# Filter sums on TensorE, a new order of the opening loads, delta gates in the low-rank products, one set of decay sums

## The chip, the cores and the metric

The kernel runs on one core of one Trainium2 chip. The metric is the device time of one execution in microseconds; less is better. TensorE (PE) multiplies, VectorE (DVE) and ScalarE (ACT) work on elements, GpSimd (POOL) here issues DMAs, and SyncE (SP) issues most of the weight loads.

## The reference, cut to what matters

256 tokens of width 1024 go through two blocks of two layers each. All is float32.

```python
def hybrid_layer(x, mem_n, ...):            # first block, layers 0 and 1
    h = rmsnorm(x, norm_mix)
    (a_x, a_b, a_c, d_q, d_k, d_v, i_q, i_k, i_w, ...) = split_cols(h @ w_in)
    y_a = a_b * causal_conv3(a_c * a_x, conv_w)
...
def ab_prepare(t, w_in, ...):               # second block, layer 0, on latent and context tokens
    gq, gk, gv, gz, ga, gb, lq, lk, lv, lg, llr = jnp.split(t @ w_in, AB_SPLITS, axis=-1)
    gate = jnp.einsum('bldr,drk->bldk', heads(llr, 2, GLA_GATE_RANK), gla_gate_w) + gla_gate_b
    gdn_g = -jnp.exp(a_log) * jax.nn.softplus(heads(ga, 2, GDN_HEADS) + dt_bias)
    gdn_beta = jax.nn.sigmoid(heads(gb, 2, GDN_HEADS))
...
def run_gdn(q, k, v, g, beta, s0, emit):    # chunks of 64 tokens
    gc = jnp.cumsum(g, axis=-1)
...
def hyena_filters(l, w1, b1, ..., filt_out):# second block, layer 1
    hdn = jnp.sin(fr * (z @ w1 + b1)); hdn = jnp.sin(fr * (hdn @ w2 + b2)); hdn = jnp.sin(fr * (hdn @ w3 + b3))
    h = (hdn @ filt_out).reshape(l, 2, HY_ORDER, D_MODEL)      # forward and backward filter
    return h * window
def long_conv(z, h_fwd, h_bwd, skip):       # two-sided, h_bwd[0] is not used
```

With a spectrum that uses the symmetry, the long convolution needs the sum and the difference of the forward and the backward filter, with row 0 of the backward one taken as zero.

## The kernel before, in words

One program per engine is written out by hand; each waits on semaphores that name what it needs (`reached("...")`), and each mark names what is done. The sources of TensorE, ScalarE and VectorE for the first block start at lines 318, 935 and 1263, for the second block at 1954, 2433 and 2702; `whole_program` (line 3232) holds SP's and POOL's lists and the short prologue of ScalarE.

Weights come in panels: `panel_plan` and `second_panels` give their order, and a ring of six slots of 1 MB holds them. A panel waits until the panels that had its slots are used. A panel of 512 columns (2 MB) takes two slots, the first three being a_x0, small0 and a_c0. Where a product is split into high and low parts, ScalarE copies the high part of a quarter panel (`prepared`) and VectorE subtracts to the low part (`lows`). `Banks.take` hands out four PSUM banks in turn; a new user waits until the old result is read.

Opening. SP issues the two tiles of x, the whole constant table (identity, masks, ones, inverse frequencies: 1.28 MB), half of the small parameter rows, positions, mem, and then the panels in their order (lines 3326 to 3345). ScalarE issues the other half of the parameter rows before it does anything else (3416). TensorE first turns the four stacks of parameter rows into columns (583), VectorE copies them (1403), and only then does the norm of x begin: sum of squares on ScalarE (950), root on VectorE (1302 to 1312), scaling (1318), transposes (556), gain (1348). Then come a_x, small (two results) and a_c. Behind the first products VectorE makes the sine table's arguments (`constants_of_dve`) and the norm of mem.

Second block, layer 0. After lv TensorE makes the low-rank rows llr of both token sets (48 rows of output) and then, with tokens as rows, the 16 columns of the delta gates (gab), for each token tile and each of eight k. lq, the gates, lk, gk and so on follow. `decays_summed(s)` multiplies gab with triangular and block matrices of ones, for each token set and tile; VectorE copies (`decays_copied`), ScalarE takes the exponential.

Second block, layer 1. Three filter layers (`filter_pe`, `filter_act`, `filter_dve`) run inside the FFN steps 4, 6 and 8 of layer 0. `filters(n)` (2334) is called after hy0 and again after hy5: for both column halves and both token tiles it makes the forward and the backward filter, with 64 rows in. `filtered(n)` (3084) on VectorE multiplies each with the window into a temporary, adds and subtracts them to hs and hd, zeroes the backward row 0 and adds the skip row. `filter_spectrum(n)` needs both; with n = 1 the spectra Z of the tokens are made between `filters` and `filter_spectrum`. POOL loads what the filters need once the attention residual of layer 0 is done (3380 to 3400) and then the modulation weights (3360).

## Time and profile before

| what | value |
| --- | --- |
| median of 3 runs | 2268.71 us (2268.51 to 2268.97) |
| profiled execution, device time | 2271.08 us |
| profiled execution, span | 2269.3 us, mean granted clock 0.975 |
| TensorE busy | 2175.8 us, 96% of the span |
| VectorE busy | 1432.4 us, 63% |
| ScalarE busy | 809.5 us, 36% |
| chain that ended last | PE 84%, DVE 10%, ACT 2%, DMA 2%, issue 1% |

A row of busy times gives the stretch and its length, then the busy us and the number of instructions of PE, PEld, DVE, ACT and POOL, the granted clock, the DMA share and GB/s.
### The profile page before, as it was taken

How to read it: one execution, taken by the hardware profiler on the slowest of the kernel's cores; microseconds unless marked ns; L12 is line 12 of the kernel's file. 1: busy time of each engine (PE TensorE's matmuls, PEld its weight loads, DVE VectorE, ACT ScalarE, POOL GpSimd, SP SyncE). 2: the span in 40 equal slices, each digit the busy share in tenths (PEclk: the TensorE clock that was granted, in tenths of full speed). 3: DMA queues.
4: the chain of work that ended last, by engine and by line, in shares of the span. 5: the costliest groups of instructions: out<-in, count | busy, mean ns of one | idle time of the engine just before them, and what ended most of it. 6: DMA issues, size and time to landing. Idle time of an engine off the chain costs nothing.

```text
span 2269.3 us, 36109 instructions
## 1 busy us (share of the span) xinstructions
PE 2175.8 (96%) x15182; PEld 1866.2 (82%) x15182; DVE 1432.4 (63%) x2369; ACT 809.5 (36%) x1026; POOL 57.4 (3%) x79
## 2 busy tenths in 40 slices
PE   6999999999999999999999998989999989999997
PEld 5997899799999878979997887886699967557996
DVE  4791677599568537758975385665477662645454
ACT  3453642334336446204442353220444312104342
POOL 0000000000000000000100000000100000000000
PEclk9999999999999989999999998998999999999999
DMA  6433347776464333777972212010686433204562
GB/s 211 178 132 129 111 166 251 235 247 215 134 193 162 130 112 112 254 266 246 300 250 84 94 56 75 2 39 1 197 278 223 149 121 111 74 10 154 181 186 74
DMA packets 207766, 348.59 MB, mean 154 GB/s; under 512 B 20642, under 2 KB 111561, under 8 KB 207220
## 3 DMA queue, kind: packets, MB, share of 16 engines
q1 hardware_dynamic: 192704, 290.89, 38.3%
q0 software_dynamic: 14624, 55.31, 7.1%
q8 instruction: 120, 1.97, 0.3%
q14 instruction: 42, 0.34, 0.1%
q10 hardware_dynamic: 276, 0.08, 0.0%
HBM read 345.21 MB, written 1.05 MB: 153 GB/s over the span
## 4 chain that ended last, share of the span: by engine, by line
PE 84%; DVE 10%; ACT 2%; DMA 2%; issue 1%; SPq 0%; POOL 0%; DVEq 0%; ACTq 0%
PE psum L447 35%; PE psum L841 29%; PE psum L484 16%; DVE G L1348 2%; DMA ring<-in_w_in_dram 1%; PE psum L819 1%; PE psum L542 1%; DVE wide_room L1348 1%; PE psum L556 1%; DMA x1tok<-in_mod_w_dram 1%; DVE x L1348 1%; DVE ring_low L1348 0%; ACT A L944 0%; DVE A L1728 0%; DVE A L1348 0%
## 5 line engine op out<-in xcount | busy, mean ns | idle before, releaser
L1218 DVE TENSOR_TENSOR ring_low<-ring,high_weights 128x2048 fp32r<-128x2048 f32 x124 | 284.3, 2292 | 132.7 <-ACT high_weights L1211 129.9
L841 PE MATMUL psum<-high_rows,high_weights 128*128 128x256 f32 x1280 | 361.6, 283 | 0.7 <-ACT xn L1239 0.7
L841 PE MATMUL psum<-high_rows,ring_low 128*128 128x256 f32 x1280 | 360.9, 282 | 0.0
L484 PE MATMUL psum<-mix_rows_high,ring_low 128*128 128x256 f32 x960 | 270.9, 282 | 0.0
L447 PE MATMUL psum<-hT,ring 128*128 128x128 f32 (+1 forms) x1552 | 255.8, 327 | 10.0 <-DVE x L1348 3.4
L447 PEld LDWEIGHTS psum<-hT,ring 128*128 128x128 f32 x1552 | 230.8, 196 | 33.6 <-issue 6.5
L841 PEld LDWEIGHTS psum<-high_rows,high_weights 128*128 128x128 f32 x1280 | 240.9, 188 | 3.5 <-issue 2.2
L841 PEld LDWEIGHTS psum<-high_rows,ring_low 128*128 128x128 f32 x1280 | 243.3, 190 | 0.0
L1211 ACT ACTIVATE high_weights<-ring 128x2048 fp32r<-128x2048 f32 x124 | 237.9, 1919 | 8.3 <-DMA ring<-in_ffn_w_dram 2.9
L484 PEld LDWEIGHTS psum<-mix_rows_high,ring_low 128*128 128x128 f32 x960 | 183.0, 191 | 0.0
L841 PE MATMUL psum<-x2T_low,high_weights 128*128 128x256 f32 x640 | 180.1, 281 | 0.0
L841 PE MATMUL psum<-yT_low,high_weights 128*128 128x256 f32 x640 | 179.8, 281 | 0.0
L1728 DVE SCALAR_TENSOR_TENSOR A<-A,silu_c 128x256 f32<-128x256 f32 x336 | 163.0, 485 | 12.0
L484 PE MATMUL psum<-mix_rows_high,work_high 128*128 128x256 f32 x560 | 160.4, 286 | 0.0
L484 PE MATMUL psum<-xn_low,work_high 128*128 128x256 f32 x560 | 156.9, 280 | 0.0
L841 PE MATMUL psum<-high_weights,high_act 128*128 128x512 f32 x352 | 140.9, 400 | 1.8 <-DVE ring_low L1218 1.4
L841 PE MATMUL psum<-ring_low,high_act 128*128 128x512 f32 x352 | 138.3, 393 | 0.0
L841 PE MATMUL psum<-high_weights,xn_low 128*128 128x512 f32 x352 | 137.5, 391 | 0.0
L841 PEld LDWEIGHTS psum<-x2T_low,high_weights 128*128 128x128 f32 x640 | 121.4, 190 | 0.5
L841 PEld LDWEIGHTS psum<-yT_low,high_weights 128*128 128x128 f32 x640 | 120.4, 188 | 0.7
L447 PE MATMUL psum<-ring,hT 128*128 128x512 f32 (+2 forms) x320 | 120.9, 529 | 0.0
L484 PE MATMUL psum<-mix_rows_high,mix_high 128*128 128x256 f32 x400 | 116.7, 292 | 3.4 <-DVE ring_low L1348 3.4
(443 smaller groups left out, 3776.2 us busy)
## 6 DMA issues: line engine op xcount, KB each, us to landing
ring<-in_w_in_dram SPq DMA_DIRECT2D x36, 2048.0 KB, 7.8
ring<-in_ffn_w_dram SPq DMA_DIRECT2D x66, 1024.0 KB, 5.4
ring<-in_ffn_w_up_dram SPq DMA_DIRECT2D x44, 1024.0 KB, 6.2
A<-in_mod_w_dram POOLq DMA_DIRECT2D x40, 1024.0 KB, 8.0
ring<-in_ffn_w_down_dram SPq DMA_DIRECT2D x22, 1024.0 KB, 4.9
ring<-in_w_lift_dram SPq DMA_DIRECT2D x16, 1024.0 KB, 9.2
ring<-in_ab_w_in_dram SPq DMA_DIRECT2D x7, 2048.0 KB, 8.2
ring<-in_hy_w_in_dram SPq DMA_DIRECT2D x6, 2048.0 KB, 8.1
```

Of the source, the lines that this page charges most:

```text
L447: return pe.eng.matmul(out, lhsT, rhs, start=(k == 0), stop=(k == n - 1))
L484: ins = pe.eng.matmul(out, lhs[a], rhs[b], start=first and n == 0, stop=last and n == 2)
L542: ins = pe.eng.transpose(b[:, i * P:(i + 1) * P], src(i), ident[:, :])
L556: ins = pe.eng.transpose(b[:, i * P:(i + 1) * P], rows[:, t, k * P:(k + 1) * P], ident[:, :])
L819: ins = pe.eng.matmul(b[:, 2 * c + which:2 * c + which + 1], mod_acc(i)[:, which, c * P:(c + 1) * P], consts["ones"][:, 0:1], start=True, ...
L841: ins = pe.eng.matmul(out, lhs[a], rhs[b], start=first and n == 0, stop=last and n == 2)
L1211: a.eng.activation(high, whole, ACT.Copy).then_inc(*a.mark(f"w_hi/{l}.{i}"))
L1218: v.eng.tensor_tensor(low, whole, high.bitcast(F32), ALU.subtract).then_inc(*v.mark(f"w_lo/{l}.{i}"))
L1348: e.tensor_tensor(dst, a, b, op).then_inc(*v.mark(label, also))
L1728: v.eng.scalar_tensor_tensor(acc, w[:, k, :], s, acc, ALU.mult, ALU.add).then_inc(*v.mark(f"mod_acc/{i}" if done else None))
```

## The change

- Filters: the third filter layer is made twice, in rows 0 to 63 and 64 to 127, the backward copy's first column is zeroed, and a second version has the lower half negated. Forward and backward filter weights lie above each other, so that one matmul with 128 rows in gives the sum and another the difference. VectorE multiplies each with the window, and adds the skip row. POOL issues three more small DMAs for the second copy.
- Opening: SP loads x tile 0, the gains of the mix norms, the identity, x tile 1, panel a_x0, half of the parameter rows, panel small0, the inverse frequencies, positions, panel a_c0, mem, the rest of the table and the other panels. ScalarE issues its half after the squares of x. TensorE turns the gains alone first, and all stacks after a_x. The constants move ahead of a_c's parts, and the norm of mem behind them.
- Delta gates: their 16 weight columns join the low-rank panel, so that the product has 80 rows of output; after lq a product with a 16 by 16 identity brings them to token rows.
- Decay sums: five matmuls for both token sets and tiles, and one set of copies and one exponential.

```diff
@@ -575,13 +575,10 @@
-        pe.wait_ge(*reached("params/all"))
-        pe.wait_ge(*reached("params_b/all"))
-        for i, n in enumerate(top["stack_rows"]):
-            label = f"stackT_ready/{i}"
-            b = take(label)
-            ins = pe.eng.transpose(b[:, 0:n], top["stacks"][0:n, i, :], ident[0:n, 0:n])
-            ins.then_inc(*pe.mark(label))
+        pe.wait_ge(*reached("gains/all"))
+        b = take("stackT_ready/gains")
+        ins = pe.eng.transpose(b[:, 0:16], top["stacks"][0:16, 0, :], ident[0:16, 0:16])
+        ins.then_inc(*pe.mark("stackT_ready/gains"))
...
@@ -604,6 +601,13 @@
+            if l == 0:
+                pe.wait_ge(*reached("params/all"))
+                pe.wait_ge(*reached("params_b/all"))
+                b = take("stackT_ready/all")
+                for i, n in enumerate(top["stack_rows"]):
+                    ins = pe.eng.transpose(b[:, i * P:i * P + n], top["stacks"][0:n, i, :], ident[0:n, 0:n])
+                ins.then_inc(*pe.mark("stackT_ready/all"))
...
@@ -629,6 +633,8 @@
+            if l == 0:
+                pe.wait_ge(*reached("table/rest"))
...
@@ -1028,14 +1034,13 @@
             if l == 0:
-                for t in range(MT):
-                    a.wait_ge(*reached(f"xn/mix0.{t}"))
-                    squared("mem", t, mem_in, "mem_in/0")
+                top["act_loads"]()
...
-            prepared(l, None, 0)
+            if l:
+                prepared(l, None, 0)
...
@@ -1043,6 +1048,9 @@
                      [f"read a_x_ready/{l}.{u}"])
             if l == 0:
                 constants_of_act()
+                prepared(l, None, 0)
+                for t in range(MT):
+                    squared("mem", t, mem_in, "mem_in/0")
             b = take(f"small_ready/{l}.0")
...
@@ -1422,24 +1424,33 @@
+                else:
+                    v.wait_ge(*reached(f"x_in_{t}/0"))
...
-                if t == 0 and l:
-                    norm_out(f"mix{l}", 0, PA[:, 8 * l:8 * l + 8])
-            for t in range(MT):
-                if t or not l:
-                    norm_out(f"mix{l}", t, PA[:, 8 * l:8 * l + 8])
+                if (l, t) == (0, 0):
+                    label = "stackT_ready/gains"
+                    e.tensor_copy(PA[:, 0:16], take(label)[:, 0:16]).then_inc(*v.mark("columns/gains", ["read " + label]))
+                    v.wait_ge(*v.own())
+                norm_out(f"mix{l}", t, PA[:, 8 * l:8 * l + 8])
...
+            if l == 0:
+                b = take("stackT_ready/all")
+                for i, n in enumerate(top["stack_rows"]):
+                    lo = 0 if i else 16
+                    e.tensor_copy(top["columns"][i][:, lo:n], b[:, i * P + lo:i * P + n]).then_inc(
+                        *v.mark(f"columns/{i}", ["read stackT_ready/all"] if i == 3 else []))
+                    v.wait_ge(*v.own())
+            if l == 0:
+                constants_of_dve()
...
-                constants_of_dve()
-                for t in range(MT):
-                    norm_rows("mem", t, mem_in)
-
+                v.wait_ge(*reached("table/rest"))
+                norm_rows("mem", 0, mem_in)
...
@@ -1451,6 +1462,8 @@
+                if l == 0 and u == 1:
+                    norm_rows("mem", 1, mem_in)
...
@@ -1927,26 +1945,36 @@
+        if i == 2:
+            v.eng.memset(hdn[FR:, 2, 0:1], 0.0).then_inc(*v.mark())
+            v.wait_ge(*v.own())
+            for rows, sign in ((slice(0, FR), 1.0), (slice(FR, P), -1.0)):
+                v.eng.tensor_scalar(hdn[rows, 3, :], hdn[rows, 2, :], sign, None, ALU.mult).then_inc(
+                    *v.mark("hdn_pairs/0" if sign < 0 else None))
+                v.wait_ge(*v.own())
...
@@ -2077,17 +2105,17 @@
-        def decays_summed(s):
-
-            pe.wait_ge(*reached(f"g/{s}"))
-            b = take(f"dec_ready/{s}")
-            for t in range(MT):
-                for d in range(2):
-                    mm(b[:, 32 * t + 4 * d:32 * t + 4 * d + 4], consts["tri"][:, d, :], gab[:, s, t, 4 * d:4 * d + 4])
-                mm(b[:, 32 * t + 8:32 * t + 16], consts["chunk_ones"], gab[:, s, t, 0:8])
-                for c in range(2):
-                    ins = mm(b[:, 32 * t + 16 + 8 * c:32 * t + 24 + 8 * c], consts["chunk_sel"][:, c, :], gab[:, s, t, 0:8])
-            ins.then_inc(*pe.mark(f"dec_ready/{s}"))
+        def decays_summed():
+
+            for s in SL:
+                pe.wait_ge(*reached(f"g/{s}"))
+            b = take("dec_ready/all")[:, 0:128].rearrange("p (s t c) -> p s t c", s=2, t=2)
+            for d in range(2):
+                mm(b[:, :, :, 4 * d:4 * d + 4], consts["tri"][:, d, :], gab[:, :, 0:2, 4 * d:4 * d + 4])
+            mm(b[:, :, :, 8:16], consts["chunk_ones"], gab[:, :, 0:2, 0:8])
+            for c in range(2):
+                ins = mm(b[:, :, :, 16 + 8 * c:24 + 8 * c], consts["chunk_sel"][:, c, :], gab[:, :, 0:2, 0:8])
+            ins.then_inc(*pe.mark("dec_ready/all"))
...
@@ -2114,16 +2142,16 @@
-                ins = mm(b[0:48, 0:SEQ], w[:, k, 16:64], src[s][:, k, :], k, KD)
-            ins.then_inc(*pe.mark(f"llr_ready/{s}"))
-        for s in SL:
-            b = take(f"gab_ready/{s}")
-            for t in range(MT):
-                for k in range(KD):
-                    ins = mm(b[:, t * 16:t * 16 + 16], src[s][:, k, t * P:(t + 1) * P], w[:, k, 0:16], k, KD)
-            ins.then_inc(*pe.mark(f"gab_ready/{s}", [used] if s else []))
+                ins = mm(b[0:80, 0:SEQ], w[:, k, 0:80], src[s][:, k, :], k, KD)
+            ins.then_inc(*pe.mark(f"llr_ready/{s}", [used] if s else []))
         w, used = panel("lqk")
         transposed("lq", w, [], 1, 2, 0)
+        for s in SL:
+            pe.wait_ge(*reached(f"llrT/{s}"))
+            b = take(f"gab_ready/{s}")
+            for t in range(MT):
+                ins = mm(b[:, t * 16:t * 16 + 16], narrow[64:80, s, t * P:(t + 1) * P], ident[64:80, 64:80])
...
@@ -2337,13 +2364,13 @@
-                    pe.wait_ge(*reached("hdn/2"))
+                    pe.wait_ge(*reached("hdn_pairs/0"))
...
-                        ins = mm(b, hdn[:, 2, t * P:(t + 1) * P], filt[:, (2 * n + half) % 2, s * HALF:(s + 1) * HALF])
+                        ins = mm(b, hdn[:, 2 + s, t * P:(t + 1) * P], filt[:, half, :])
...
@@ -2556,7 +2583,7 @@
-            copy(llrT[:, s, :], take(f"llr_ready/{s}")[0:48, 0:SEQ], f"llrT/{s}", [f"read llr_ready/{s}"])
+            copy(narrow[:, s, :], take(f"llr_ready/{s}")[0:80, 0:SEQ], f"llrT/{s}", [f"read llr_ready/{s}"])
...
@@ -2588,9 +2615,8 @@
-        for s in SL:
-            a.wait_ge(*reached(f"dec/{s}"))
-            copy(decx[:, s, :, :], decx[:, s, :, :], f"decx/{s}", func=ACT.Exp)
+        a.wait_ge(*reached("dec/all"))
+        copy(decx[:, :, :, :], decx[:, :, :, :], "decx/all", func=ACT.Exp)
...
@@ -2811,14 +2837,14 @@
+        def decays_copied():
+
+            label = "dec_ready/all"
+            e.tensor_copy(dec[:, :, :, :], take(label)[:, 0:128].rearrange("p (s t c) -> p s t c", s=2, t=2)).then_inc(*v.mark(None, ["read " + label]))
...
-            e.tensor_copy(decx[:, s, :, :], dec[:, s, :, :]).then_inc(*v.mark())
+            e.tensor_copy(decx[:, :, :, :], dec[:, :, :, :]).then_inc(*v.mark())
             v.wait_ge(*v.own())
-            tt(decx[:, s, :, 8:16], dec[:, s, :, 8:16], dec[:, s, :, 0:8], ALU.subtract, f"dec/{s}")
+            tt(decx[:, :, :, 8:16], dec[:, :, :, 8:16], dec[:, :, :, 0:8], ALU.subtract, "dec/all")
...
@@ -3089,16 +3114,11 @@
-                    tt(tmp2[:, 0, :], take(l0), window[:, t, cc], ALU.mult, None, ["read " + l0])
-                    tt(tmp2[:, 1, :], take(l1), window[:, t, cc], ALU.mult, None, ["read " + l1])
-                    if t == 0:
-                        e.memset(tmp2[0:1, 1, :], 0.0).then_inc(*v.mark())
-                        v.wait_ge(*v.own())
-                    tt(hs[:, t, cc], tmp2[:, 0, :], tmp2[:, 1, :], ALU.add)
+                    tt(hs[:, t, cc], take(l0), window[:, t, cc], ALU.mult, None, ["read " + l0])
                     if t == 0:
                         tt(hs[0:1, 0, cc], hs[0:1, 0, cc], skip[0:1, n, cc], ALU.add)
-                    tt(hd[:, t, cc], tmp2[:, 0, :], tmp2[:, 1, :], ALU.subtract, f"filtered/{n}.{half}.{t}",
-                       [f"h_sums/{n}"] if half and t else [])
+                    tt(hd[:, t, cc], take(l1), window[:, t, cc], ALU.mult, f"filtered/{n}.{half}.{t}",
+                       ["read " + l1] + ([f"h_sums/{n}"] if half and t else []))
...
@@ -3322,18 +3342,8 @@
-            for t in range(MT):
-                sp.eng.dma_start(x[:, t, :], io["x"][0][t * P:(t + 1) * P, :]).then_inc(*sp.loads(f"x_in_{t}/0"))
-            sp.eng.dma_start(const_sb[:, :], io["shape_table"]).then_inc(*sp.loads("const/ident"))
-            for dst, src in loads_of_params[0::2]:
-                sp.eng.dma_start(dst, src).then_inc(*sp.loads(f"params/{len(marks.at)}"))
-            sp.eng.dma_start(top["pos"][:, :], io["positions"][0].partition_broadcast(P)).then_inc(*sp.loads("pos/0"))
-            for l in range(DEPTH):
-                sp.eng.dma_start(top["gb_out"][:, l, :], io["hgrn_out_norm"][l].partition_broadcast(P)).then_inc(*sp.loads(f"pos/gb{l}"))
-            marks.at["params/all"] = ("params", marks.count["params"])
-            marks.at["pos/all"] = ("pos", marks.count["pos"])
-            sp.eng.dma_start(first["mem_in"], io["mem"][0].rearrange("(t p) d -> p t d", p=P)).then_inc(*sp.loads("mem_in/0"))
...
@@ -3341,6 +3351,28 @@
+            sp.eng.dma_start(x[:, 0, :], io["x"][0][0:P, :]).then_inc(*sp.loads("x_in_0/0"))
+            for dst, src in gains_of_mix:
+                sp.eng.dma_start(dst, src).then_inc(*sp.loads(f"gains/{len(marks.at)}"))
+            marks.at["gains/all"] = ("gains", marks.count["gains"])
+            sp.eng.dma_start(const_sb[:, 0:P], io["shape_table"][:, 0:P]).then_inc(*sp.loads("const/ident"))
+            sp.eng.dma_start(x[:, 1, :], io["x"][0][P:2 * P, :]).then_inc(*sp.loads("x_in_1/0"))
+            panel_asked(plan[0])
+            for dst, src in loads_of_params[0::2]:
+                sp.eng.dma_start(dst, src).then_inc(*sp.loads(f"params/{len(marks.at)}"))
+            panel_asked(plan[1])
+            sp.eng.dma_start(const_sb[:, -2:], io["shape_table"][:, -2:]).then_inc(*sp.loads("pos/inv_freq"))
+            sp.eng.dma_start(top["pos"][:, :], io["positions"][0].partition_broadcast(P)).then_inc(*sp.loads("pos/0"))
+            for l in range(DEPTH):
+                sp.eng.dma_start(top["gb_out"][:, l, :], io["hgrn_out_norm"][l].partition_broadcast(P)).then_inc(*sp.loads(f"pos/gb{l}"))
+            marks.at["params/all"] = ("params", marks.count["params"])
+            marks.at["pos/all"] = ("pos", marks.count["pos"])
+            panel_asked(plan[2])
+            sp.eng.dma_start(first["mem_in"], io["mem"][0].rearrange("(t p) d -> p t d", p=P)).then_inc(*sp.loads("mem_in/0"))
+            sp.eng.dma_start(const_sb[:, P:-2], io["shape_table"][:, P:-2]).then_inc(*sp.loads("table/rest"))
+            for name in plan[3:]:
+                panel_asked(name)
...
@@ -3384,8 +3416,11 @@
+            pool.eng.dma_start(second["hyw"][:, 3, :], io["hy_pos_w3_2"][0]).then_inc(*pool.loads("params3/w2_again"))
+            pool.eng.dma_start(second["hyb"][FR:, 2:3], io["hy_pos_b3_2"][0].rearrange("(p a) -> p a", a=1)).then_inc(*pool.loads("params3/b2_again"))
+            for s in range(2):
+                pool.eng.dma_start(second["hyb"][s * FR:(s + 1) * FR, 3:4], io["hy_freq_2"][0].rearrange("(p a) -> p a", a=1)).then_inc(*pool.loads(f"params3/freq{s}"))
...
@@ -3412,9 +3447,13 @@
-            for dst, src in loads_of_params[1::2]:
-                act.eng.dma_start(dst, src).then_inc(*act.loads(f"params_b/{len(marks.at)}"))
-            marks.at["params_b/all"] = ("params_b", marks.count["params_b"])
+            def act_loads():
+
+                for dst, src in loads_of_params[1::2]:
+                    act.eng.dma_start(dst, src).then_inc(*act.loads(f"params_b/{len(marks.at)}"))
+                marks.at["params_b/all"] = ("params_b", marks.count["params_b"])
+
+            top["act_loads"] = act_loads
...
```

## Rows read from the trace of the kernel before

**Rows 1.** Chain of waits in order of time: start us, us, what.
```profile
11.32 13.74 DMA ring<-in_w_in_dram
```

**Rows 2.** Busy time in two stretches of the opening.
```profile
25.11:53.77 28.66, 28.66 (x201) 27.83 (x202) 16.19 (x37) 13.30 (x20) 0.00 (x0) 1.00 0.59 179
15.00:20.00 5.00, 1.17 (x4) 0.65 (x4) 3.50 (x15) 0.00 (x0) 0.00 (x0) 1.00 0.99 387
```

**Rows 3.** Timeline, opening: start us, us, engine line op, [idle before <-releaser].
```profile
8.18 1.28 ACT L950 ACT_TABLE_LOAD   x1 [8.18 <-issue]
...
9.48 1.06 ACT L950 ACTIVATE yT<-x 128x1024 f32<-128x1024 f32 x1
...
15.41 1.17 PE L583 MATMUL psum<-const_sb,ytok 104*128 104x104 f32 x4 [15.41 <-DMA ytok<-in_hy_conv_w_dram]
...
17.13 0.15 DVE L1302 TENSOR_SCALAR st<-st 128x1 f32<-128x1 f32 x1
...
20.02 1.97 PE L556 MATMUL psum<-const_sb,xn 128*128 128x128 f32 x8 [3.43 <-DVE xn L1318]
...
22.86 1.42 DVE L1348 TENSOR_TENSOR hT<-psum,columns 128x512 f32<-128x512 f32 x2
...
43.47 0.29 DVE L1409 CAST A<-pos 128x256 f32<-128x256 int32 x1
...
49.89 0.17 DVE L1352 TENSOR_SCALAR lbc<-lbc 128x8 f32<-128x8 f32 x1 [2.26 <-ACT lbc L1001]
```

**Rows 4.** Timeline, TensorE, projections of the second block.
```profile
1259.28 3.75 PE L447 MATMUL psum<-ring,cT 128*128 128x16 f32 x32
1262.87 6.68 PE L447 MATMUL psum<-ring,hT 128*128 128x16 f32 x32
1269.39 9.16 PE L447 MATMUL psum<-hT,ring 128*128 128x256 f32 x32
1278.48 1.14 PE L447 MATMUL psum<-row,gla_w 16*128 16x256 f32 x8
1279.55 7.17 PE L447 MATMUL psum<-cT,ring 128*128 128x256 f32 x32
```

**Rows 5.** Busy time and granted clock (PEclk) in three stretches, columns as in rows 2.
```profile
1263.00:1273.00 10.00, 10.00 (x42) 9.28 (x42) 1.05 (x6) 0.00 (x0) 0.00 (x0) 0.51 0.01 2
...
1848.00:1851.00 3.00, 2.13 (x5) 0.78 (x4) 2.70 (x6) 0.00 (x0) 1.07 (x2) 0.89 1.05 406
...
1953.00:1963.00 10.00, 8.75 (x10) 3.35 (x11) 9.40 (x15) 0.00 (x0) 0.00 (x0) 0.50 0.02 5
```

**Rows 6.** Timeline, TensorE, decay sums and gq.
```profile
1374.84 7.80 PE L447 MATMUL psum<-gab,const_sb 128*128 128x4 f32 x40 [1.48 <-DVE G L1348]
1382.48 15.84 PE L447 MATMUL psum<-hT,ring 128*128 128x256 f32 x64
```

**Rows 7.** Timeline, first filter pass.
```profile
1848.78 1.42 DVE L1348 TENSOR_TENSOR tmp<-psum,window 128x512 f32<-128x512 f32 x2
...
1853.04 1.42 DVE L1348 TENSOR_TENSOR tmp<-psum,window 128x512 f32<-128x512 f32 x2
1853.78 3.78 PE L447 MATMUL psum<-filt,hdn 64*128 64x512 f32 x4 [1.11 <-DVE tmp L1348]
...
1857.49 4.78 PE L447 MATMUL psum<-hT,ring 128*128 128x256 f32 x14
```

**Rows 8.** Timeline, second filter pass.
```profile
1957.96 16.46 PE L447 MATMUL psum<-ztok,dft 128*128 128x512 f32 x32
...
1964.26 1.42 DVE L1348 TENSOR_TENSOR wide_room<-psum,wide_room 128x512 f32<-128x512 f32 x2 [0.72 <-PE psum L447]
```

**Rows 9.** Chain of waits, FFN of the second block's first layer.
```profile
1632.13 12.80 DMA x1tok<-in_mod_w_dram
```

**Rows 10.** Instructions on the tile x before 12 us: issue to landing.
```profile
DMA to landing us min/median/max: 3.8/4.2/4.6
```

**Rows 11.** Timeline, VectorE, decay gates of the second block.
```profile
1287.89 2.04 DVE L1353 TENSOR_SCALAR G<-psum,columns 128x256 f32<-128x256 f32 x4 [4.87 <-PE psum L447]
```

61 lines of the change are left out of this document (29 added, 32 removed).

## The prediction, made before the changed kernel was run

> **What bounds the kernel now.** I read the chain of waits first, then the timelines of the stretches that the diff touches, then the granted clock in them. The chain lies on TensorE nearly throughout, so an edit pays in two cases only: where it takes instructions off TensorE while TensorE is what the chain follows, or where it shortens a stretch in which TensorE stands. In order of time the change touches five places.
>
> The opening. The chain begins with a weight load: the panel a_x0 is issued at 11.32 and lands 13.74 us later [rows 1], and from 25.11 TensorE is busy without a gap until a_c at 53.77 [rows 2]. SP has issued x, the table and half of the small parameter rows before it. The first normed tile is there earlier, when TensorE's transposes start at 20.02 [rows 3].
>
> The gates of the second block. TensorE spends 3.75 + 6.68 us on matmuls of 16 columns, and the lq product behind them takes 9.16 us where the equal lk product takes 7.17 [rows 4]. The granted clock is 0.51, the lower level of 1.2 GHz, from 1263 to 1273, and TensorE has been busy all the time before it fell, with these narrow matmuls [rows 4, 5].
>
> The decay sums. Forty records of 4 to 8 columns take 7.80 us, and gq's 64 records behind them 15.84 us [rows 6]; twice the 7.17 of lk [rows 4] would be 14.3.
>
> The filters, twice. TensorE gets four results out, has to wait for a bank, and VectorE reads a bank only every other pair of its own instructions [rows 7, 8]. Here too the clock goes to 0.50 [rows 5].
>
> The modulation load behind POOL's row of small DMAs, 12.80 us in the chain [rows 9].
>
> **The change part by part.**
>
> Opening. TensorE's first product needs the first half of hT for tile 0 and the panel a_x0. After the change the path to hT is: x tile 0 lands 3.8 us after its issue at 0.74, at 4.5 [rows 10]. ScalarE no longer issues 19 DMAs first; it loads its table (1.28) and squares (1.06, and about 0.1 for reading the sum) [rows 3]: 7.0. The root and the scaled copy on VectorE are the stretch from 17.13 to the transposes at 20.02, 2.9 us [rows 3]: 9.9. Four transposes are half of 1.97, and one of the two gain multiplies half of 1.42 [rows 3]; with three hand-overs of some 0.07: 11.8. VectorE copies the gains while TensorE transposes. ScalarE issues its 19 DMAs after its second square and is done near 15; only its high copies of hT queue behind them, which nobody needs before a_c. The panel has 0.5 + 0.06 + 0.5 + 2 MB of x, identity and itself to pass. The queue moved 387 GB/s when it was full [rows 2]; 3.1 MB are 8.0 us from about 2.5, so it lands near 10.6 to 11.5, just ahead of hT. I take 11.9 for the start against 25.11: 13.2 us less.
>
> The four transposes of the parameter stacks, which lay in idle time, now stand between a_x and small. They took 1.17 us at the low clock [rows 3], 0.6 at the full one, and behind them TensorE waits, by my estimate, 0.15 for ScalarE to read a_x's second bank. That is 0.75 back: the opening gives 12.4.
>
> What could eat it is the work that the new order puts behind TensorE's start: the sine table, the parameter columns and the mem norm. Between start and a_c TensorE has 28.66 us of work of its own, VectorE 16.2 and ScalarE 13.3 in the same time [rows 2], so both have room. But the order in it changes: ScalarE makes the high parts of a_c only behind its constants, which need the four columns. The stacks are turned some 19 us after the start (a_x is about two thirds of the 28.66, then the 0.75); the copies took about 1.1; from the cast at 43.47 to the answer to the sigmoid are 6.4 us [rows 3]; the first part then needs a copy and a subtraction, some 2.3. That makes 28.8 us after the start, and TensorE asks at 29.4. It is close, so I keep 1 us of stall for the range. VectorE's wait for the rest of the table holds mem's norm and, behind it, the copy of dvw and the products of a_c; the table is the seventh large thing on SP's queue, 0.5 + 0.5 + 2 + 1.3 + 2 + 1 + 1.2 MB, some 28 us by the rate of [rows 2] with allowance for the narrow rows of small, and VectorE asks at about 44. Bounds for the opening: 9 (start at 14.3, 1 us of stall) to 14.
>
> Delta gates. Removed: 3.75 + 6.68 us, less overlap 1259.28 to 1269.39, 10.1 us [rows 4]. The clock no longer has this reason to fall, so lq takes 7.17 and not 9.16: 2.0 more. The product that carries them now has 80 output rows instead of 48 and the same 256 columns; a product with 128 rows of output takes 7.17/32 = 0.22 us a record, so the wider one costs nothing [rows 4]. Added: four matmuls, 8 records, with 16 rows in; the nearest row is the 8 records 16*128 of 256 columns, 1.14 us [rows 4], which bounds it above; I take 0.8. Where the path goes: VectorE waits for TensorE at 1287.89, by 4.87 us [rows 11], and then works on until TensorE waits for it, so it must start earlier too. VectorE's six operations on the gates of 16 columns now fall right before the first of these, beside the gate matmuls that it needs anyway. 12.1 - 0.8 = 11.3. Bounds 9 and 12.1. The panel small2 has one DMA more, which lands under lv's matmuls. The low-rank copy on ScalarE is done while lq runs, so the wait on it costs nothing; lq is the cover, and without it the copy would lie bare. Queued behind TensorE's wait are the gates of the context.
>
> The Trainium skill speaks against this part (TensorE: Matmul & The Clock Gate, section LDWEIGHTS): the time to load weights goes by their columns. By that, 32 columns more in 32 loads would cost 0.9 us if the loads were the limit. The record spacing in [rows 4] says that the moving side is.
>
> Decay sums. 40 records become 10. At the spacing of the 40, 7.80/40, they take 1.95: 5.85 less [rows 6]. TensorE is the chain here, and gq follows. VectorE and ScalarE have half the operations (some 0.6 us) and lie behind gq. Bounds: 4 (the clock recovers only as late as now, and gq pays) and 6.5. I take 5.8.
>
> Filters, VectorE. Each of the eight pairs loses an add, a subtract becomes the second multiply, and the temporary with its memset goes. The pair with t = 0 takes 4.26 us now (1848.78 to 1853.04), the one with t = 1 2.9; at 0.72 an instruction they take 2.2 and 1.45 after [rows 7]. All four: 14.3 against 7.3. **First pass.** The fifth matmul waits for the same read as now, at 1849.5. The seventh waits for the first read of t = 1, at 1853.75 now and at 1851.7 after. At the full clock, 0.86 us a matmul, the eight are out at 1853.6 instead of 1857.49: 3.9 us [rows 7]. What follows is TensorE's own. **Second pass.** VectorE itself is the chain: it ends the filters 7.0 us earlier, and the next thing it waits for are the first two spectra, out at 1964.26 now [rows 8]. By the same steps the eighth matmul ends at 1954.05. The 16 spectrum matmuls take 16.46 us, of which 5 at half clock [rows 5, 8], so 0.86 each; two spectra of two end at 1957.6: 6.6 us. Sum 10.5. If the clock falls as it does now, the last matmuls and the first spectra take twice as long, and the first pass gives 0.7 and the second 1.5. The filter sum now has 128 rows in instead of 64; the columns and so the time are the same.
>
> Filter layer and POOL. Layer 3 has a memset and two scalings more on VectorE, under 1 us inside an FFN step in which it has idle time. POOL issues three DMAs more ahead of the filters and the modulation load, about 0.52 us each. The load behind is 12.8 us long for 1 MB [rows 9] against 13.74 for 2 MB behind 1 MB of mem in the opening [rows 1]: its queue is behind, not its issue, so 1.6 us of issue are mostly hidden. I take 0.7, bounds 0 and 1.8.
>
> Sum: 12.4 + 11.3 + 5.8 + 10.5 - 0.7 = 39.3 us. The profiled span is 2269.3 and the device time of that execution 2271.08; the span after is 2230.0 and its time 2231.8. The median of the three runs is 2268.71, 2.4 below the profiled one, so 2229.4.
>
> **The rivals.**
>
> Clock: the pauses in the filters remain (0.9 and 0.5 us), and the clock falls as now. For it: it fell at 1851 after pauses no longer than these, with TensorE busy 2.13 of 3 us [rows 5]. Against: those matmuls used half of the rows. The filters then give 2.2: 31.0 in all, 2237.7. The Trainium skill (same page, A second HAM failure mode: psum-queue depth-cycling) has this as its rule: short idles between groups that cycle through the banks send the clock down again and again.
>
> Opening held by loads: a_x0 shares the engines with ScalarE's parameter rows and small's narrow ones, or the constants keep a_c waiting. With the start at 17 us it gives 7.3: 34.2 in all, 2234.5. The 13.74 of a 2 MB panel in [rows 1] is for it, the 387 GB/s of [rows 2] against it.
>
> Gates: the saving on TensorE is not followed by VectorE's chain, because something else (the gk panel, ScalarE's table loads) becomes late. At half of 11.3: 2235.
>
> Slower: the rest of the table lands late, VectorE stands at its wait, and everything it owes to a_b stops TensorE. To turn the sum it would have to land at about 58 + 39.3, near 97 us, on a queue with nothing to wait for ahead of it but issue. That gives 2273 or more from a landing at 102.
>
> Not doing what it says: should the narrow matmuls not be on the chain at all, [rows 11] would show VectorE busy at their end; it is idle.
>
> **How the numbers follow.** Forecast 0.62, clock 0.15, opening 0.12, gates 0.07, slower 0.03, no change 0.01. The lower end of the range takes the upper bounds of opening and clock phases (14 + 12 + 6.3 + 12, 2225) and 2 for clock changes elsewhere: 2223. The upper end covers the clock rival and half of another: 2241. A measurement here can tell about 0.2% from no change, 4.5 us; all but the last two cases are far beyond.
>
> **What would show it.** First matmul of a_x near 12; no gap before a_c; no 16-column stretch and clock 1.00 in lq; ten records of decay sums; VectorE 2.2 and 1.45 a pair in the filters, and the first product of Z near 6.6 us earlier in its stage; the modulation's first multiply no later against the residual before it. Wrong would be a start beyond 15, a VectorE wait on the table, or 0.50 in the filters for as long as now.

## The result

| kernel | median, us | range | ratio to before, 95% interval |
| --- | --- | --- | --- |
| before (beside it) | 2268.84 | 2268.51 to 2270.45, 4 runs | |
| changed | 2236.36 | 2232.31 to 2240.38, 4 runs | 0.985 [0.9832, 0.9867] |

The change gives 32.5 us, 1.4%. The forecast was 2229.4 with a range of 2223 to 2241: right in sign, inside the range, 7 us too low. The profiled execution is the quickest of the four: 2232.31 us, span 2230.4 (forecast 2231.8 and 2230.0), mean granted clock 0.984 against 0.975. The share of the clock that was not granted, times the span, says how much full-speed time TensorE was short of: it falls from 56.7 to 35.7 us, so up to 21 us of the 38.8 between the two traces is clock and not instructions taken away.

The page of the changed kernel, busy time of each engine and the share of the chain that ended last by engine:

```profile
PE 2147.5 (96%) x15097; PEld 1846.8 (83%) x15097; DVE 1419.7 (64%) x2350; ACT 808.7 (36%) x1025; POOL 59.1 (3%) x82
...
PE 83%; DVE 11%; ACT 3%; DMA 1%; issue 1%; POOL 0%; SPq 0%; DVEq 0%; ACTq 0%
```

TensorE lost 28 us of busy time and 11 us of standing. The rows that answer to those ahead of the prediction follow, place by place.

**Opening** (to rows 1 to 3). The chain of waits, from its start, then the timeline (start, duration, engine, line and operation, in brackets the idle time before and who ended it):

```profile
2.78 9.54 DMA ring<-in_w_in_dram
12.36 7.93 PE psum L447 x48
...
0.73 1.28 ACT L956 ACT_TABLE_LOAD   x1 [0.73 <-PEq L3487]
...
4.27 1.06 ACT L956 ACTIVATE yT<-x 128x1024 f32<-128x1024 f32 x1 [2.25 <-DMA x<-in_x_dram]
...
9.72 0.69 DVE L1356 TENSOR_TENSOR hT<-psum,columns 128x512 f32<-128x512 f32 x1 [1.07 <-PE psum L556]
...
30.94 7.14 PE L447 MATMUL psum<-hT,ring 128*128 128x256 f32 x32 [0.25 <-ACT work L950]
```

The first product starts at 12.36 instead of 25.11, and what starts it is the landing of a_x0: half of hT is there at 10.41, 1.95 us before. a_c starts at 41.61 instead of 53.77.

**Gates** (to rows 4, 11). Timeline of TensorE: the low-rank product of the context has 80 output rows; lq, the four small matmuls and the gate products follow without a narrow stretch. The last row is VectorE's.

```profile
1240.85 3.62 PE L447 MATMUL psum<-cT,ring 128*80 128x256 f32 x16
1244.31 10.52 PE L447 MATMUL psum<-hT,ring 128*80 128x256 f32 x48
1254.76 0.72 PE L447 MATMUL psum<-const_sb,row 16*128 16x16 f32 x5
...
1256.63 7.17 PE L447 MATMUL psum<-cT,ring 128*128 128x256 f32 x32
...
1264.97 2.04 DVE L1361 TENSOR_SCALAR G<-psum,columns 128x256 f32<-128x256 f32 x4 [4.90 <-PE psum L447]
```

**Decay sums** (to rows 6), timeline of TensorE. Ahead of gq there is a wait that the kernel before doesn't have:

```profile
1350.40 1.30 PE L447 MATMUL psum<-gab,const_sb 128*128 128x16 f32 x10 [1.48 <-DVE G L1356]
1352.79 16.95 PE L447 MATMUL psum<-hT,ring 128*128 128x256 f32 x64 [1.09 <-DVE G L1356]
```

**Filters** (to rows 5, 7, 8): timeline of the first pass, then busy time and granted clock (PEclk, the number before the DMA share) in both stretches:

```profile
1817.92 3.75 PE L447 MATMUL psum<-filt,hdn 128*128 128x512 f32 x8
1822.58 1.10 PE L447 MATMUL psum<-filt,hdn 128*128 128x512 f32 x2 [0.91 <-DVE wide_room L1356]
1823.93 2.84 PE L447 MATMUL psum<-filt,hdn 128*128 128x512 f32 x6 [0.25 <-DVE wide_room L1356]
1826.61 13.98 PE L447 MATMUL psum<-hT,ring 128*128 128x256 f32 x64
...
1816.00:1831.00 15.00, 13.84 (x56) 8.58 (x55) 11.55 (x21) 0.60 (x1) 2.10 (x4) 1.00 0.53 175
1912.00:1930.00 18.00, 16.66 (x41) 7.45 (x41) 13.98 (x23) 0.60 (x1) 0.00 (x0) 1.00 0.37 117
```

The clock no longer falls in either pass, and a matmul of 512 columns (two records) takes 0.9 us through both.

### The profile page after: what moved, and what is told of

The parts are those of the page before. It is cut to its first block, busy times and chain, and to the rows that moved or that the text cites. A ratio compares the mean times of both kernels' runs of the same rounds, so it can differ in the third digit from the quotient of the medians.

```text
span 2230.4 us, 35917 instructions
## 1 busy us (share of the span) xinstructions
PE 2147.5 (96%) x15097; PEld 1846.8 (83%) x15097; DVE 1419.7 (64%) x2350; ACT 808.7 (36%) x1025; POOL 59.1 (3%) x82
## 3 DMA queue, kind: packets, MB, share of 16 engines
q1 hardware_dynamic: 194056, 290.96, 38.8%
q8 instruction: 119, 1.95, 0.4%
## 4 chain that ended last, share of the span: by engine, by line
PE 83%; DVE 11%; ACT 3%; DMA 1%; issue 1%; POOL 0%; SPq 0%; DVEq 0%; ACTq 0%
PE psum L447 34%; PE psum L847 30%; PE psum L484 16%; DVE G L1356 2%; DMA ring<-in_w_in_dram 1%; PE psum L825 1%; PE psum L542 1%; DVE wide_room L1356 1%; PE psum L556 1%; DVE ring_low L1356 1%; DVE x L1356 1%; DMA x1tok<-in_mod_w_dram 0%; DVE A L1356 0%; ACT A L950 0%; DVE A L1741 0%
## 5 line engine op out<-in xcount | busy, mean ns | idle before, releaser
L447 PE MATMUL psum<-yT,ring 128*128 128x256 f32 x512 | 115.7, 379 | 0.0
```

The costliest lines, as they stand in the source:

```text
L447: return pe.eng.matmul(out, lhsT, rhs, start=(k == 0), stop=(k == n - 1))
```

## The leads, place by place

To say where time goes I set the start of the same VectorE instruction in two traces side by side and call the difference the lead. All leads here are against the second trace of the kernel before (label before_again, an execution of 2266.04 us), whose own times head the rows. "first" is the trace of the kernel before on which the prediction rests.

```
us   first opening gates decays decays filters changed whole  rows64 pauses panel_  split_ split_
           _only   _only _only  _again _only           _again               and_gq  and_gq only
100  -0.9   11.4   -0.4  -0.2    0.3    0.1    11.3   10.0   10.6   10.5   11.2    13.6   10.0
300  -4.1    7.1   -4.2  -0.3   -1.4    0.1     9.7    7.4    9.0    8.8    9.5    10.2    5.8
900  -5.4    5.9   -2.2  -0.3   -2.8    0.1     5.9    7.6    7.7    7.3    8.3     8.8    2.3
1290 -5.4    5.9    9.4  -0.3   -2.8    0.1    17.5   19.2   19.3   19.0   19.9    20.4   13.9
1352 -5.3    6.0    9.4  -0.3   -2.7    0.1    19.2   19.2   19.3   19.0   19.9    20.4   15.5
1425 -5.2    6.1    9.2   3.5    1.1    0.1    22.7   24.6   24.8   24.5   28.4    28.9   19.1
1550 -5.1    6.0    9.7   3.1    0.6    0.2    24.8   25.0   25.4   21.7   22.4    22.9   18.6
1810 -4.7    6.1   11.4   2.4   -2.2    0.3    22.3   26.3   27.1   23.2   24.0    24.7   19.8
1850 -4.8    6.1   11.4   2.1   -3.2    5.5    27.5   31.6   28.9   25.2   29.2    29.9   23.8
1935 -5.0    6.1   10.4   0.9   -4.6    5.5    27.5   31.6   28.9   25.2   29.2    29.9   23.8
1980 -5.1    6.1   11.0   1.5   -4.0   11.9    33.9   37.9   31.6   25.8   35.5    36.3   30.2
2260 -5.0    5.9   11.0   0.0   -5.7   11.9    33.9   36.3   30.1   25.6   34.0    36.3   30.2
```

A part of the change is a step between two rows: the opening is row 100, the gates lie between 900 and 1290, the decay sums between 1352 and 1425, the filters between 1810 and 1850 and between 1935 and 1980. The gates (11.6 to 11.7) and, with 128 rows and without VectorE's old work, the filters (5.2 to 5.3 and 6.3) take the same step in every trace that has the part, but for split_only's first pass (4.0, of which a low stretch ahead of the filter matmuls, 0.66 from 1800 to 1810, takes 1.2); the decay sums (3.5 to 5.6, 8.6 with gq moved) and the opening (10.0 to 13.6) don't. What the table shows outside the steps comes and goes between traces of one and the same kernel. One such piece helps the change: from 1290 to 1352 the column "changed" gains 1.7 us, where both traces of the kernel before have a short low stretch of the clock (0.89 from 1300 to 1315) and this one has none (1.00 from 1280 to 1300).

## The experiments

**1. The kernel before, again.** No edit.

> The kernel before once more, for a second trace of it. Against its first trace every difference is the spread of one and the same kernel. Theory 'clock': the leads wander by 3 to 5 us where the low stretches of the clock lie elsewhere (200 to 300 and 790 to 850 first of all), the stretches without a low clock take the same time within 0.1 us, and the falls at the narrow matmuls (1263) and in both filter passes (1850, 1953) are there again.

2266.04 us. The two traces of one kernel are 5 us apart, and the column "first" shows where: 3.2 us from 100 to 300, 1.3 from there to 900, nothing to speak of in the remaining 1360. The busy time and clock of two stretches, in the first trace and then in the second, hold both:

```profile
190.00:250.00 60.00, 54.90 (x251) 42.66 (x251) 19.00 (x26) 23.42 (x38) 0.00 (x0) 0.86 0.30 107
780.00:850.00 70.00, 63.92 (x306) 50.88 (x306) 21.98 (x34) 27.10 (x43) 0.00 (x0) 0.88 0.34 120
...
190.00:250.00 60.00, 55.77 (x275) 43.57 (x276) 21.64 (x37) 25.30 (x40) 0.00 (x0) 0.92 0.30 105
780.00:850.00 70.00, 63.93 (x330) 51.57 (x329) 27.24 (x43) 27.55 (x43) 0.00 (x0) 0.90 0.31 112
```

Same work, less clock. The fall at the narrow matmuls (9.39 us for lq in this trace) and those in the filter passes are there in both. The executions of the kernel before that ran beside the experiments lie between 2265.94 and 2274.76 us, their medians between 2269.03 and 2271.77. So the prediction's base, 2268.5 to 2269.0, looked firmer than it was.

**2. The four parts, each alone.** Each is the kernel before with the hunks of one part of the diff shown earlier.

```diff
 opening_only:  every hunk on DMA order, gains, stacks, constants_of_dve, prepared
 gates_only:
+    ins = mm(b[0:80, 0:SEQ], w[:, k, 0:80], src[s][:, k, :], k, KD)
+    ins = mm(b[:, t * 16:t * 16 + 16], narrow[64:80, s, t * P:(t + 1) * P], ident[64:80, 64:80])
 decays_only:
+    mm(b[:, :, :, 8:16], consts["chunk_ones"], gab[:, :, 0:2, 0:8])
 filters_only:
+    ins = mm(b, hdn[:, 2 + s, t * P:(t + 1) * P], filt[:, half, :])
```

> Only the new opening on top of the kernel before. In the two traces a_c starts 12.16 us earlier, and behind it the lead wanders: 13.8 at 186, 11.3 from 868 on. Theory 'own price': the opening gives what it gives at a_c, 12.2 us, so 2256.6; first product of a_x at 12.4, right after the landing of a_x0. Theory 'clock on top': the later low stretches of TensorE's clock move when everything starts 12 us earlier; then the span differs from 12.2 by up to 3 us either way, and the difference is seen in the product (1 - granted clock) x span, which is 56.7 us in the trace before.

2259.57 us (2256.28 to 2260.69), ratio 0.9954 [0.9939, 0.9969] to 2270.2 beside it: 10.6 us. The lead is 11.4 at a_c (12.2 over the first trace, as expected) and 5.9 at 900. The first product starts at 13.13, with the landing of a_x0, not at 12.4. Between 100 and 900 it loses 5.5 us, about what the first trace of the kernel before loses there (4.5). "Clock on top" holds: the clock not granted, times the span, is 56.5 us here and 49.8 in before_again, 6.7 us more.

> Only the delta gates as rows of the low-rank product. Theory 'narrow matmuls': the matmuls of 16 columns brought the clock down, so without them it stays at 1.00 through lq, lq takes 7.2 us, and the change gives 12.5 us as in the trace of the whole change: 2256.3. Theory 'stretch': the clock falls in this stretch for what lies before it (lv, the pauses at 1223 to 1250) and would fall in this kernel too at some place from lv to lk; then lq or lk takes 9 to 14 us and the change gives about 10: 2258.8.

2256.26 us (2255.05 to 2260.98), 0.9946 [0.9931, 0.9961]: 13.9 us. The step is 11.6 us (-2.2 to 9.4), the same 11.6 as with the whole change (5.9 to 17.5), and the clock stays up where it fell. The first two lines are this kernel, the last two the second trace of the kernel before:

```profile
1252.00:1262.00 10.00, 10.00 (x48) 8.12 (x47) 0.00 (x0) 0.76 (x2) 0.00 (x0) 1.00 0.44 168
1262.00:1275.00 13.00, 13.00 (x71) 10.55 (x70) 5.98 (x15) 5.96 (x6) 0.00 (x0) 1.00 0.01 2
...
1252.00:1262.00 10.00, 10.00 (x65) 8.99 (x64) 0.52 (x3) 0.38 (x1) 0.00 (x0) 0.80 0.20 75
1262.00:1275.00 13.00, 13.00 (x53) 10.81 (x54) 1.17 (x5) 0.60 (x1) 0.00 (x0) 0.76 0.01 2
```

"Stretch" falls: nothing ahead of the low-rank product is changed, and only the narrow matmuls are gone. The fall is in all six traces that have them and in none of the eight that don't. The 12.5 us that I had put in this expectation is too much for the step. Between the traces of the kernel before and the changed kernel it is 11.6 too up to 1290, and 13.1 up to 1352, the short low stretch near 1306 included.

> Only the decay sums for all tiles at once. Theory 'VectorE is late': with 10 records instead of 40 gq asks for its bank before VectorE has read it, and stands about 1.1 us (the trace of the whole change has 1.09), and the clock rises as late as before, so that gq takes about 17 us; 4.2 us less in all: 2264.6. Theory 'TensorE only' (the prediction's sum): no wait ahead of gq and gq no longer than 15.8: 5.8 us less, 2263.0.

2271.8 us (2264.69 to 2276.7, ten executions), 1.0007 [0.9994, 1.002]: nothing, although its trace (2266.16 us) shows a step of 3.7. Both theories on the size are about the trace alone. There "VectorE is late" is right: gq has 1.08 us of wait ahead of it and takes 16.82. That the median shows nothing was in neither. A second trace:

> The kernel with the decay sums alone, once more, for a second trace of it. In the first, taken in an execution of 2266.2 us, the lead grew by 3.6 us in the decay sums and the granted clock was 0.975; but six of its ten executions had 0.972 and took 2271.6 to 2276.7 us. Theory 'clock elsewhere': an execution at 0.972 has the same 3.5 us of lead in the decay sums and loses some 9 us at other places, where the clock is low and was not in the first trace. Theory 'clock behind the sums': the change itself brings the clock down longer in the stretch from the sums to the delta rule (1371 to 1430), and the lead there is gone. If this execution is one at 0.975, it decides nothing but shows the spread of the leads.

```profile
1374.72 16.76 PE L447 MATMUL psum<-hT,ring 128*128 128x256 f32 x64 [0.99 <-DVE G L1348]
...
1640.00:1655.00 15.00, 12.43 (x63) 10.81 (x62) 14.28 (x19) 5.69 (x4) 0.88 (x1) 0.77 1.00 336
1815.00:1835.00 20.00, 16.61 (x96) 14.79 (x96) 12.86 (x34) 4.38 (x9) 0.00 (x0) 0.83 0.59 211
2055.00:2070.00 15.00, 12.88 (x70) 9.88 (x69) 8.05 (x26) 3.52 (x8) 0.00 (x0) 0.89 0.42 140
```

2271.71 us at a clock of 0.972, one of the common kind. The step is there again (-2.7 to 1.1, 3.8 us), so "clock behind the sums" falls. From 1425 on the lead goes from 1.1 to -5.7. Some 5.7 of these 6.8 us go in the three stretches, all far from the edit, and most of the rest in the first filter pass, where the clock is low in the kernel before too. In both traces of the kernel before the clock is 1.00 in all three; in both traces of decays_only it is below (0.89, 0.91, 0.89 in the first). So this is no mere chance of one execution. By what the edit brings them, the runs don't show. It isn't the earlier start by itself: opening_only is 6 us ahead at these places and has none of the three, and decays_again has all three although it reaches 1640 only 0.6 us ahead of before_again.

> Only the filter sums on TensorE, with the third filter layer, its scalings and POOL's three more DMAs. Theory 'shorter pauses keep the clock': clock 1.00 in both stretches of filter matmuls, 5.4 us less in the first pass, 6.4 in the second, and up to 1.5 of it given back in the FFN before (POOL's DMAs, the filter layer): 2257.0 to 2258.5. Theory 'chance': that the clock stayed up in the trace of the whole change hung on when the stretch began; here it falls to 0.5 in at least one of the passes, and the change gives 6 to 9 us: 2260 to 2263.

2257.96 us (2254.14 to 2259.78), 0.9947 [0.9932, 0.9962]: 12.2 us. This trace and the second one of the kernel before agree within 0.15 us for the first 1480 us, where the code is the same: when the clock is low at the same places, nothing else varies. The steps are 5.2 and 6.3 us, clock 1.00 in both passes. POOL's three more DMAs and the longer filter layer cost nothing: 0.1 at 1425, 0.3 at 1810. "Shorter pauses" forecast the numbers, but the next two runs show that it isn't the reason that the clock stays up.

The four medians add up to 10.6 + 13.9 - 1.6 + 12.2 = 35.1 us; each is uncertain by some 3.

**3. Rows or pauses: what holds the clock in the filters.**

```diff
 rows64 (the backward filter is left out of the result):
-    ins = mm(b, hdn[:, 2 + s, t * P:(t + 1) * P], filt[:, half, :])
+    ins = mm(b, hdn[0:FR, 2 + s, t * P:(t + 1) * P], filt[0:FR, half, :])
 pauses (VectorE, behind the two multiplies of a pair):
+    tt(tmp2[:, 0, :], hs[:, t, cc], hd[:, t, cc], ALU.add)
+    if t == 0: e.memset(tmp2[0:1, 1, :], 0.0)
+    tt(tmp2[:, 1, :], hs[:, t, cc], hd[:, t, cc], ALU.subtract, ...)
```

> The changed kernel, but each filter matmul uses the first 64 of its 128 rows only (the forward filter alone; the backward filter is left out of the result). Number, columns and order of all instructions stay. Theory 'shorter pauses': the granted clock stays 1.00 in both stretches of filter matmuls (around 1818 to 1842 and 1913 to 1940), the eight matmuls take the same time and the span is that of the changed kernel within the spread. Theory 'more rows': it was the use of all 128 rows that held the clock; with 64 it falls to 0.5 for about 10 us in both passes, and the span grows by 4 to 5 us in the first pass and by 1 to 5 in the second.

> The changed kernel with VectorE's work of before put back as idle operations: per pair one addition and one subtraction into a temporary behind the two multiplies, and the memset for the first token tile, so that TensorE waits for its banks as before. 128 rows. Theory 'shorter pauses': the clock falls to 0.5 for about 10 us in both passes as before, and the whole gain of the filters goes, 11.9 us. Theory 'more rows': the clock stays 1.00 and only VectorE's own time comes back: about 2 us in the first pass (4.26 and 2.9 us a pair again, TensorE at full clock) and 6 to 7 in the second, where VectorE is the chain: 8 to 9 us.

First rows64, timeline and stretches, then pauses:

```profile
1813.17 3.70 PE L447 MATMUL psum<-filt,hdn 64*128 64x512 f32 x8
1817.73 1.09 PE L447 MATMUL psum<-filt,hdn 64*128 64x512 f32 x2 [0.87 <-DVE wide_room L1356]
1819.08 4.45 PE L447 MATMUL psum<-filt,hdn 64*128 64x512 f32 x6 [0.26 <-DVE wide_room L1356]
...
1816.00:1831.00 15.00, 13.88 (x38) 8.05 (x37) 7.71 (x12) 0.00 (x0) 2.10 (x4) 0.77 0.43 152
1912.00:1930.00 18.00, 16.85 (x31) 6.35 (x30) 11.85 (x20) 0.48 (x1) 0.00 (x0) 0.81 0.38 117
```

```profile
1821.65 1.96 PE L447 MATMUL psum<-filt,hdn 128*128 128x512 f32 x4 [0.90 <-DVE wide_room L1356]
1825.83 1.98 PE L447 MATMUL psum<-filt,hdn 128*128 128x512 f32 x4 [2.22 <-DVE wide_room L1356]
1828.82 14.05 PE L447 MATMUL psum<-hT,ring 128*128 128x256 f32 x64 [1.01 <-DVE wide_room L1356]
...
1816.00:1831.00 15.00, 10.87 (x37) 5.57 (x36) 13.26 (x24) 0.60 (x1) 2.10 (x4) 1.00 0.52 175
1912.00:1930.00 18.00, 13.78 (x39) 6.93 (x38) 12.94 (x23) 0.60 (x1) 0.00 (x0) 1.00 0.37 117
```

With nearly the pauses of the changed kernel (0.87 and 0.26 us against its 0.91 and 0.25) but 64 rows the clock falls, and six records take 4.45 us instead of 2.84. With 128 rows and longer pauses (0.90, 2.22, 1.01) it stays at 1.00. "More rows" is right and "shorter pauses" wrong: in this place the clock hangs on how many rows the matmuls use. Each of the two runs is a single trace, but the others agree: all seven traces whose filter matmuls use 64 rows have the low stretch in both passes, and all seven with 128 rows have it in neither. The fall in rows64 is shorter than expected, some 7 us a pass instead of 10, and costs 3.6 in each instead of 4 to 5 and 1 to 5. The times are 2236.13 and 2240.4 us. The steps split the gain: VectorE's shorter work with a falling clock (rows64) gives 1.7 and 2.8 us in the two passes, the clock with VectorE's old work (pauses) 2.0 and 0.6, and both together 5.2 and 6.3. The old work takes 9.0 us back, where 8 to 9 were expected. Each is worth most when the other is there: VectorE's saving shows only while TensorE is quick enough to need the banks sooner.

**4. The changed kernel, again.** No edit.

> The changed kernel once more, with more runs. Theory 'clock on top': the steps of the change are worth 39 us in every run, and what is missing to that in the median (32.5) is TensorE's clock at other places, in other runs at others: time and (1 - granted clock) x span go together, with 2237 near 45 us of loss and 2232 near 36; the profile shows the same leads of 11.6 us in the gates, 3.5 in the decay sums, 5.4 and 6.4 in the filters. Theory 'steps vary': the steps themselves give less in most runs, and the clock loss doesn't follow the time.

2236.9 us (2229.86 to 2238.63), 0.9855 [0.9836, 0.9875]: 32.1 us. Time and (1 - clock) x span go together: 2229.86 with about 35.6 us, 2236.08 with 40.2, 2237.72 and 2238.63 with 44.7 each. The traced execution is again the quickest, and its steps are 10.0, 11.6, 5.4, 5.3 and 6.3, in all 38.6. The first product starts at 14.06 here: a_x0 took 11.23 us to land. Steps of 38 to 39 us, and a time that follows the clock: the first theory, with one correction, that the decay sums and the opening vary by 2 us by themselves. Where the clock is low in the slower executions no trace shows, because both traces are of quick ones.

**5. Two further edits.**

```diff
 panel ahead of tile 1 (panel_and_gq):
+            panel_asked(plan[0])
             sp.eng.dma_start(x[:, 1, :], ...)
-            panel_asked(plan[0])
 gq ahead of the decay sums (panel_and_gq, split_and_gq):
-        decays_summed()
         w, used = panel("gq")
         transposed("gq", w, [used], 1)
+        decays_summed()
 a_x0 in two requests (split_and_gq, split_only):
+            sp.eng.dma_start(room[:, :, 0:SEQ], src[:, :, 0:SEQ]).then_inc(*sp.loads("a_x_first/0"))
             sp.eng.dma_start(x[:, 1, :], ...)
+            sp.eng.dma_start(room[:, :, SEQ:], src[:, :, SEQ:]).then_inc(...)
```

> The changed kernel with two edits: a_x0 is requested ahead of the second tile of x, and the decay sums stand behind gq (VectorE copies them behind its last convolution, ScalarE takes their exponential together with the gates'). Theory 'panel bounds the start, VectorE bounds gq': the first product starts at 10.5 to 10.8 instead of 12.36, when hT of tile 0 is there (10.4), and gq starts at its bank, without the pauses of 1.48 + 1.09 us both; 1.7 + 1.1 = 2.8 us less at both places, 2233.6 if the clock elsewhere is alike. Rival 'the second tile is late': x of tile 1 lands behind 2 MB, near 13.5 to 14 us, its hT comes after 20, and TensorE stands in a_x by as much as it gained; rival 'exponential late': the decays are copied only at 1373 and the pause goes to the first chunk of the delta rule, so that gq's 1.1 us is given back.

2234.24 us (2232.22 to 2237.91), 0.9843 [0.9824, 0.9862]. The start stays at 12.35: now a_x0 is requested at 2.30 and takes 10.01 us, and tile 1 of x comes at 13.6. Half a megabyte less ahead of it brings the panel no earlier: the transfers share the engines, and now x waits instead. "Panel bounds the start" is right on what is waited for, but the edit doesn't shorten it. TensorE doesn't stand for tile 1 either, so that rival is out too. At gq the edit does more than was expected:

```profile
1349.81 14.05 PE L447 MATMUL psum<-hT,ring 128*128 128x256 f32 x64 [1.57 <-DVE G L1356]
1363.69 1.20 PE L447 MATMUL psum<-gab,const_sb 128*128 128x16 f32 x10
```

The second wait is gone, the clock doesn't fall (14.05 us for the 64 records, which took 15.65 to 16.95 in every trace that has the sums ahead of gq), and the step of the decay sums is 8.6 us instead of 3.5 to 5.6. So "exponential late" isn't seen up to there. But from 1425 to 1550 6.0 us of lead are lost. 3.75 of them go in one group of 128 records, which take 13.39 us instead of 9.64 where the clock is at 0.52 (1496 to 1506); 2.0 go just before it, where every kernel with the change loses 1 to 2.

> The changed kernel; a_x0 now comes in two requests of 256 columns each, the first ahead of the second tile of x and TensorE waiting for it alone, the second behind that tile; and the decay sums behind gq as in the run before. Theory 'landing of 2 MB bounds the start': the first MB lands near 8, so the first product starts at 10.4 to 10.6, when hT of tile 0 is there, and no longer varies (12.35 to 14.06 in the five traces with the new opening); the lead over the kernel before is 13.4 to 13.6 us at a_c instead of 10.8 to 12.2. With 3.1 us at gq the time is 2236.9 - 2 - 3.1 = 2231.8. Rival 'bandwidth': TensorE then stands before the second half of the columns or at tile 1 for as long as it started earlier, and a_c starts no earlier than 41.6; 2233.8. Rival for gq: what it gains at gq is lost to the clock by 1550, as in the run before (33.65 us of lead at 1480, 27.6 at 1550): 2235.

2230.87 us (2229.32 to 2234.88), 0.983 [0.9811, 0.9849]. The chain now begins with x, not with the panel:

```profile
0.74 3.84 DMA x<-in_x_dram
4.60 1.16 ACT yT L962 x2
8.77 1.97 PE psum L556 x8
10.84 6.92 PE psum L447 x48
```

The start is at 10.84, the lead at a_c 13.6. That shows what bounded the start: the landing of the 2 MB. The decay sums give 8.6 us and 6.0 are lost again from 1425 to 1550, as in the run before.

> The changed kernel with a_x0 in two requests alone; the decay sums stand where the change put them. Theory 'place': moving gq forward is what brought the low stretch of 13.7 us at 1492 in both kernels that had it (6 us of lead lost from 1480 to 1550); here it isn't there, the lead grows by 3.5 to 5.5 us in the decay sums and keeps it through the delta rule. The start is 10.6 to 10.9 again and the lead at a_c 13.3 to 13.6. By that the time is no more than that of the kernel with both edits, 2230.9, and 2 to 4 us under the changed kernel's 2236.9: 2231 to 2235 by the start alone. Rival 'chance': the low stretch at 1492 comes here too, and the time is 3.1 us over that of both edits: 2234.

2236.01 us (2227.84 to 2240.03), 0.9843 [0.9824, 0.9863]. The start is at 10.87 again, but the lead at 100 is 10.0, not 13.6, and the loss from 1425 to 1550 is 0.5. "Place" has its point on the low stretch (there in both kernels with gq moved, not here; one more kernel, pauses, lost 2.9 us there too, so it isn't tied to gq alone). It is wrong on the time. ScalarE's row shows what is next in the opening:

```profile
47.63 1.06 ACT L956 ACTIVATE work_high<-ring 128x1024 fp32r<-128x1024 f32 x1 [3.64 <-DMA ring<-in_w_in_dram]
```

The fourth panel lands at 47.2 us, 19.4 after its request, and everything behind a_c waits. With both edits ScalarE waited 1.76 us for the same panel, without harm; in the changed kernel it doesn't wait. The two kernels have the same code up to gq, so the 3.6 us between their leads at 100 is spread from execution to execution. With this order of loads the fourth panel comes so close behind that, by these two traces, an earlier start would gain little more than the 13.6 us of the run before. None of the three variants is shown to beat the changed kernel: their intervals overlap its own. The one with both edits has the lowest median, 2230.87.

## Why the prediction was right, and where it was off

Point by point, the forecast's terms against the steps of the two traces of the changed kernel:

| term | forecast | measured |
| --- | --- | --- |
| opening, at a_c | 12.4 | 11.3 and 10.0 (12.2 and 10.8 over the first trace) |
| delta gates | 11.3 | 11.6, three times |
| decay sums | 5.8 | 3.5 and 5.4 |
| filters | 3.9 + 6.6 | 5.2 + 6.3 |
| filter layer, POOL | -0.7 | 0 |
| sum | 39.3 | 38 to 38.6 |
| median | 39.3 | 32.5 and 32.1 |

**Opening.** The size was nearly right for two wrong reasons. ScalarE loads its table at 0.73, while x is still on its way, and not behind the landing; so half of hT is there at 10.4 and not at 11.8. And a_x0 doesn't land at 10.6 to 11.5 but at 12.3 to 14.0. The step that failed is the rate: 387 GB/s from 2.5 us on. The changed kernel's trace has 150 GB/s from 1 to 3 us, 228 from 3 to 5, and at the end, when small parameter rows and the narrow rows of small0 come in beside and behind the panel's last ones, the engines are busy and move half:

```profile
9.00:11.00 2.00, 1.47 (x7) 1.07 (x6) 1.11 (x2) 0.00 (x0) 0.00 (x0) 1.00 1.05 383
11.00:13.00 2.00, 0.64 (x3) 0.64 (x4) 1.72 (x9) 0.00 (x0) 0.00 (x0) 1.00 0.97 193
```

That is the rival "opening held by loads", at 0.5 to 2.2 us instead of the 5.1 of a start at 17. The stacks' term was sized from a wrong reading: their 1.17 us was taken for the low clock, but the granted clock is 1.00 there ([rows 2]). TensorE was slower at its start in a way that this column doesn't show, as the eight transposes of either tile of x do in the changed kernel, both at a granted clock of 1.00:

```profile
8.50 1.97 PE L556 MATMUL psum<-const_sb,xn 128*128 128x128 f32 x8 [2.58 <-DVE xn L1326]
...
20.13 1.04 PE L556 MATMUL psum<-const_sb,xn 128*128 128x128 f32 x8
```

So the stacks take 0.75 instead of 0.6 and the bank 0.25 instead of 0.15; with the overlap the two cost 0.8 (a_x ends at 30.11, small starts at 30.94), where 0.75 was forecast. The other estimates held: the low half of a_c's first part ready 0.4 us before TensorE asks (0.6), the rest of the table never waited for: issued at 23.84, 15.5 us under way, asked for at 44.85. So the rival that ended slower had 5 us of room at the very start of its chain.

**Gates.** Right in each step: lq at the full clock, VectorE's wait unchanged (4.90 against 4.87), the stage earlier by the whole sum. The section LDWEIGHTS of the Trainium skill's page TensorE: Matmul & The Clock Gate has the load's time go by its columns; 16 records take 3.62 us with 80 columns and 3.62 with 48 (from 1250.33, second trace of the kernel before), so here that cost lies under the matmuls, as the forecast had it.

**Decay sums.** "TensorE is the chain here" failed. It is only because forty records take 7.8 us; with ten, gq asks for a bank that VectorE reads 1.09 us later. And gq still meets a low clock. The lower bound of 4 counted the clock but not the wait; 3.5 is below it. No run has the whole change without this part, and alone it gives nothing in the median, so whether it earns any of the 32.5 us is open.

**Filters.** VectorE's pairs take 2.16 and 1.45 us, as forecast. "What follows is TensorE's own" was the miss, in the good direction: in the kernel before the clock stayed low into the hy product ([rows 7]: 14 records in 4.78 us, 0.34 each, against 13.98/64 = 0.22 after), another 1.3 us in the step. The clock rival was rightly rejected, and by the right argument, the rows: had the sum used 64 rows it would have come true (7.1 us less of gain in rows64; it was priced at 8.3). The rule of the Trainium skill, same page, section A second HAM failure mode: psum-queue depth-cycling, is not borne out as the cause: in pauses TensorE stands for a bank ahead of every group of the first pass but the first, and the clock is 1.00. The range's lower end took 12 for the filters, for which no bound was worked out, and 6.3 for the decay sums, whose bound was 6.5; the filters' 11.5 lies under it.

**The median.** This is the real miss, 7 us, and it lies between the trace and the median: the profiled execution was forecast at 2231.8 and took 2232.31. I took the distance between the two, 2.4 us in the kernel before, over to the changed kernel, and let the range have 2 us for clock changes elsewhere. But the profiled execution of before, 2271.08, is an ordinary one among the 42 that ran beside the experiments (2265.94 to 2274.76, median 2270.3), and those of the changed kernel are the lowest of their four: its median lies not 2.4 below but 4.1 and 7.0 above the trace. That the forecast for the trace hit within 1 us is partly luck as well: the same trace is 38.8 us ahead of the first trace of the kernel before and 33.7 ahead of the second.

The difference of the medians is 6 us less than the steps. One place of it is seen: all eight traces with the new opening lose 2.4 to 5.5 us (split_only 7.7) between 100 and 900 against before_again, where the others lose between nothing (decays_only, filters_only) and 4.5. The loss behind the decay sums is shown for the kernel with that part alone, and not for the whole change: whole_again keeps its lead there. Which low stretches the common, slower executions of the changed kernel have is open: both of its traces are of quick ones.

## What to carry to other kernels

Follow each saved microsecond to the next reader of the buffer: the saving in the decay sums ended at a bank that nobody had waited for, and that of the opening at the next landing. Before a narrow or a half-used matmul is judged by its own duration, look at the granted clock in it and behind it: removing the 16-column matmuls also gave lq back its 2 us (7.17 instead of 9.16), and using all 128 rows kept the filters at full clock in spite of longer pauses. And take two traces of the kernel before, where a profiled execution can differ from the next by 5 us at places that no edit touches; what one trace calls a saving there may be the clock alone.

## What was not expected of the hardware

- Matmuls of 512 columns with 64 rows in: clock 0.77 and 0.81 over the two filter stretches (rows64); the same with 128 rows: 1.00, with pauses as long or longer (0.87 and 0.26 us against 0.90, 2.22 and 1.01, run pauses).
- Where the low stretches of the clock are the same, two traces of different kernels agree within 0.15 us over 1480 us; where they aren't, one kernel differs from itself by 5 us.
- With the decay sums alone changed, at 1370, both traces have low stretches at 1645, 1825 and 2060 that neither trace of the kernel before has.
- The first eight transposes of the changed kernel take 1.97 us, the next eight 1.04, with a granted clock of 1.00 in both places: the column doesn't show what slows TensorE at its start.
- ScalarE's table load of 1.28 us ran at 0.73, ahead of the wait of the instruction that needs it, which itself started at 4.27.
- The DMA engines were 97% busy at 193 GB/s from 11 to 13 us, with small parameter rows and the end of a weight panel under way, against 383 to 408 GB/s from 5 to 11, where large transfers carried nearly all of it.
